# First loads of a two-block transformer kernel: which queue issues what, and when the small loads go out

## The reference

```
cos, sin = rope_tables(positions, HEAD_DIM)
mod = einsum('bd,ldm->lbm', silu(c), w_mod) + b_mod
for i in range(2):
    sh_m, sc_m, g_m, sh_f, sc_f, g_f = split(mod[i], 6)
    h = x * (1 + sc_m) + sh_m
    y = even_mixer(h, cos, sin, ...) if i == 0 else odd_mixer(h, cos, sin, ...)
    x = layer_norm(ALPHA * x + (1 + g_m) * y, ...)
    h = x * (1 + sc_f) + sh_f
    x = layer_norm(ALPHA * x + (1 + g_f) * swiglu(h, ...), ...)
```

## Time and profile before

| | us |
|---|---|
| median of 3 runs | 1142.61 (1140.88 to 1143.27) |
| the profiled execution, device time | 1144.01 |
| its span in the profile | 1142.7 |
| TensorE busy | 1124.9 (98%) |
| VectorE busy | 842.5 (74%) |
| ScalarE busy | 627.6 (55%) |
| GpSimd busy | 81.1 (7%) |
| loads through SP's queue | 230.32 MB |
| loads through GpSimd's queue | 0.31 MB |

### The profile page before, as it was taken

How to read it: one execution, slowest core, us unless ns; L and a number is a source line. 1 busy time by engine, 2 the same in 40 slices (tenths; PEclk the granted TensorE clock), 3 DMA queues, 4 the chain that set the end, 5 groups by cost and what they waited for, 6 DMA issues and landing times.

```text
span 1142.7 us, 24990 instructions
## 1 busy us (share of the span) xinstructions
PE 1124.9 (98%) x10534; PEld 1079.2 (94%) x10534; DVE 842.5 (74%) x1429; ACT 627.6 (55%) x1075; POOL 81.1 (7%) x103
## 2 busy tenths in 40 slices
PE   8999999999999999999999999999999999999998
PEld 6998799999998999999999999999999999999987
DVE  5698879988876888897575589578565677676643
ACT  3467556645435588666444455734645566555542
POOL 3000013000012000111000034100000000000000
PEclk9999999999999999999999999999999999999999
DMA  9977755899997643566655642843345463655540
GB/s 322 381 235 275 245 176 180 301 327 306 313 313 242 202 148 116 182 217 219 219 185 166 212 149 75 259 149 113 109 150 185 148 221 102 213 189 183 197 170 37
DMA packets 194687, 232.22 MB, mean 203 GB/s; under 512 B 4083, under 2 KB 169555, under 8 KB 194576
## 3 DMA queue, kind: packets, MB, share of 16 engines
q1 hardware_dynamic: 193984, 230.32, 60.6%
q0 software_dynamic: 592, 0.31, 0.2%
HBM read 229.56 MB, written 1.05 MB: 202 GB/s over the span
## 4 chain that ended last, share of the span: by engine, by line
PE 91%; DVE 4%; DMA 2%; issue 1%; ACT 1%; POOL 0%; SPq 0%; DVEq 0%
PE ps L154 90%; PE ps L157 2%; DMA XR<-in_x_dram 1%; DVE hL L196 1%; DVE wlo L187 1%; DMA raw<-in_w_in_even_dram 1%; DVE T L187 1%; DMA MW<-in_w_mod_dram 0%; DVE LT L187 0%; DVE T L196 0%; POOL T L187 0%; DVE XA L193 0%; DVE MR L196 0%; DVE ST L199 0%; ACT RD L166 0%
## 5 line engine op out<-in xcount | busy, mean ns | idle before, releaser
L187 DVE TENSOR_TENSOR wlo<-raw,whi 128x1024 fp32r<-128x1024 f32 (+1 forms) x346 | 409.9, 1206 | 162.3 <-ACT whi L166 161.0
L154 PE MATMUL ps<-hH,whi 128*128 128x256 f32 (+3 forms) x1792 | 517.2, 289 | 2.2 <-DVE hL L196 1.9
L154 PE MATMUL ps<-hH,wlo 128*128 128x256 f32 (+3 forms) x1792 | 504.6, 282 | 1.1 <-DVE wlo L187 1.1
L154 PE MATMUL ps<-hL,whi 128*128 128x256 f32 (+3 forms) x1792 | 505.0, 282 | 0.0
L166 ACT ACTIVATE whi<-raw 128x1024 fp32r<-128x1024 f32 (+1 forms) x346 | 349.5, 1033 | 193.3 <-PE ps L154 131.7
L154 PEld LDWEIGHTS ps<-hH,whi 128*128 128x128 f32 x1792 | 337.8, 189 | 8.8 <-issue 4.5
L154 PEld LDWEIGHTS ps<-hH,wlo 128*128 128x128 f32 x1792 | 338.1, 189 | 1.3 <-DVE wlo L187 1.3
L154 PEld LDWEIGHTS ps<-hL,whi 128*128 128x128 f32 x1792 | 338.4, 189 | 0.4
L154 PE MATMUL ps<-uL,whi 128*128 128x256 f32 x352 | 99.2, 282 | 0.0
L154 PE MATMUL ps<-uH,whi 128*128 128x256 f32 x352 | 99.0, 281 | 0.0
L154 PE MATMUL ps<-uH,wlo 128*128 128x256 f32 x352 | 98.4, 280 | 0.0
(11 more groups left out here) (314 smaller groups left out, 1614.4 us busy)
## 6 DMA issues: line engine op xcount, KB each, us to landing
MW<-in_w_mod_dram SPq DMA_DIRECT2D x47, 1024.0 KB, 6.9
raw<-in_w_up_dram SPq DMA_DIRECT2D x44, 1024.0 KB, 5.5
raw<-in_w_in_dram SPq DMA_DIRECT2D x36, 1024.0 KB, 5.0
raw<-in_w_down_dram SPq DMA_DIRECT2D x27, 1024.0 KB, 6.2
raw<-in_w_gate_dram SPq DMA_DIRECT2D x22, 1024.0 KB, 7.3
raw<-in_w_in_odd_dram SPq DMA_DIRECT2D x12, 1024.0 KB, 7.3
raw<-in_w_in_even_dram SPq DMA_DIRECT2D x8, 1024.0 KB, 9.6
raw<-in_w_down_dram SPq DMA_DIRECT2D x8, 768.0 KB, 6.7
```

Of the source, the lines that this page charges most:

```text
L154: return self.queued(self.e.matmul(out, lhsT, rhs, start=start, stop=stop, skip_group_check=True, **kw), length if pos is None else max(le ...
L187: return self.queued(self.e.tensor_tensor(out, a, b, op), 0.07 + cols(out) / self.RATE)
```

## The change

It has four parts. First, the loads of the vector, the identity and the bias are issued by ScalarE's queue (`k.act_dma`, a loader on the scalar engine) ahead of its table load, so SP's first instruction is the first modulation tile. Second, GpSimd's loads wait: the positions for the arrival of modulation tile 3, the meta tokens and the 16 parameter rows for tile 5. Third, the rotary tables are no longer written in one piece before the input is turned; they are a track that starts when the positions' load has been issued and yields between groups of instructions, so that they fall among the steps of `even`. Fourth, a `pace` ahead of the switch to the exponential table set makes sure that both sines are in the program before it, and `vectors` waits until the parameter rows have been issued.

```diff
 def begin(k):
-    pos_in = pool.dma(m.PI, D_["positions"].to_broadcast([128, S]), k.into["pos"])
-    k.meta_in = pool.dma(m.MTR, D_["meta_tokens_2"], k.into["meta"])
+    k.rows_in = k.meta_in = k.rope_tables = None
...
-    for g, r, src in rows_:
-        k.rows_in = pool.dma(RV[r:r + src.shape[0], g, 0:src.shape[1]], src, k.into["rows"])
-    c_in = sp.dma(RV[0:8, 0, :], vec(D_["c"]), k.into["c"])
-    ident_in = sp.dma(m.CST[:, 0:K_TRI], D_["cst"][:, 0:K_TRI], k.into["ident"])
-    bm_in = sp.dma(RV[0:96, 1, :], vec(D_["b_mod"]), k.into["bm"])
+    c_in = k.act_dma.dma(RV[0:8, 0, :], vec(D_["c"]), k.into["c"])
+    ident_in = k.act_dma.dma(m.CST[:, 0:K_TRI], D_["cst"][:, 0:K_TRI], k.into["ident"])
+    bm_in = k.act_dma.dma(RV[0:96, 1, :], vec(D_["b_mod"]), k.into["bm"])
...
+    def late_loads():
+        while 3 not in k.mod_loaded:
+            yield None
+        yield due(k.mod_loaded[3])
+        pos_in = pool.wait_ge(*k.mod_loaded[3]).dma(m.PI, D_["positions"].to_broadcast([128, S]), k.into["pos"])
+        start(k, rope_tables(pos_in))
+        while 5 not in k.mod_loaded:
+            yield None
+        yield due(k.mod_loaded[5])
+        k.meta_in = pool.wait_ge(*k.mod_loaded[5]).dma(m.MTR, D_["meta_tokens_2"], k.into["meta"])
+        for g, r, src in rows_:
+            rows_in = pool.dma(RV[r:r + src.shape[0], g, 0:src.shape[1]], src, k.into["rows"])
+        k.rows_in = rows_in
+
+    def rope_tables(pos_in):
+        ang, turns, r = m.ANG
...
+        yield due(pos_in)
+        dve.wait_ge(*pos_in).wait_ge(*ident_in).copy(ang, m.PI).settle().ts(ang, ang, inv, ALU.mult)
+        for out, turn_ in ((m.SIN, 0.0), (m.COS, 0.25)):
+            yield dve.clock
...
+            angle = dve.settle().ts(r, r, -3.1415925, ALU.max).inc()
+            yield due(angle)
+            sine = act.wait_ge(*angle).act(out, r, ACT.Sin, scale=sgn if out is m.SIN else 1.0).inc()
+        k.rope_tables = sine
...
+    start(k, late_loads())
     start(k, centred())
 def vectors(k, lane):
...
+    while k.rows_in is None:
+        yield None
     yield due(k.rows_in, k.meta_in)
 def even(k):
...
+    pace(k, lambda: due(k.rope_tables) if k.rope_tables else None)
     k.mods_soon = 8
     k.act.table(SET_EXP)
 def program(nc, args, out):
...
+        k.act_dma = Loader(nc.scalar, None)
```

More of the change, by code:

```diff
@@ L744, in begin @@
     k.b_mod = dve.inc()
[L746 to L760, removed]
@@ L761, in begin @@
-    k.rope_tables = sine
+    def late_loads():
[11 more added lines that the diff above has]
+        k.rows_in = rows_in
@@ new lines, in rope_tables @@
+    def rope_tables(pos_in):
+        ang, turns, r = m.ANG
+        inv, sgn = m.CST[:, K_INV:K_INV + 1], m.CST[:, K_SGN:K_SGN + 1]
+        sine = None
+        yield due(pos_in)
+        dve.wait_ge(*pos_in).wait_ge(*ident_in).copy(ang, m.PI).settle().ts(ang, ang, inv, ALU.mult)
+        for out, turn_ in ((m.SIN, 0.0), (m.COS, 0.25)):
+            yield dve.clock
+            dve.settle().ts(turns, ang, 1.0 / TWO_PI, ALU.mult, turn_, ALU.add)
+            dve.settle().ts(turns, turns, MAGIC, ALU.add).settle().ts(turns, turns, -MAGIC, ALU.add)
+            yield dve.clock
+            dve.settle()
+            if sine:
+                dve.wait_ge(*sine)
+            dve.stt(r, turns, -C1, ang, ALU.mult, ALU.add)
+            yield dve.clock
+            dve.settle().stt(r, turns, -C2, r, ALU.mult, ALU.add).settle().stt(r, turns, -C3, r, ALU.mult, ALU.add)
+            yield dve.clock
+            dve.settle().ts(r, r, turn_ * TWO_PI, ALU.add, 3.1415925, ALU.min)
+            angle = dve.settle().ts(r, r, -3.1415925, ALU.max).inc()
+            yield due(angle)
+            sine = act.wait_ge(*angle).act(out, r, ACT.Sin, scale=sgn if out is m.SIN else 1.0).inc()
+        k.rope_tables = sine
```

## The result

| | before | after |
|---|---|---|
| median, us | 1142.33 (1140.88 to 1143.27) | 1150.38 (1148.07 to 1152.81, 4 runs) |
| ratio, 95% interval | | 1.0074 [1.0061, 1.0086] |
| profiled execution, us | 1144.01 | 1148.07 |
| its span, us | 1142.7 | 1146.8 |

The changed kernel is slower by 0.7%, outside the predicted range. A second measurement of it gave 1150.01 against 1142.39, 1.0069 [1.0054, 1.0084]. The profiled execution of after is the fastest of its four, the one of before lay over its median, so the spans of the two traces differ by only 4.1 of the 8 us. One execution of a later kernel, h2, took 1360.71 us at a mean granted clock of 0.751 and is left out of that kernel's ratio.

A forecast was written before the change was run, and what follows sets the result against it. TensorE, busy 1124.9 of 1142.7 us, was taken as the bound, with a late useful start. Terms -1.2 - 1.0 + 0.4 + 0.2 = -1.6 took 1142.6 to 1141.0 us; range 1138.8 to 1144.2.

The forecast's parts named there:

- SP begins earlier, GpSimd's loads leave the head: At the start: SP issues 1.33 us earlier, GpSimd's absence gives 1.0; input lands at 13.2 (12.2 to 14.2).
- TensorE's own queue set the transposes: At the head: TensorE's queue, not the input's landing, sets the transposes' start, 14.06 instead of 15.55; at most 1.49 us gained.
- The delay of the identity: At the head: identity delayed 0.3 us beside the large loads (0 to 1.7); transposes start at 14.4, term -1.2.
- the transpose of `c` after 4: Sign at the head: `c` transposed after 4 us would show the first term wrong.
- The second gain: Between input transposes and first triple: both `LT` made once copies are; triple at T + 5.1 instead of T + 6.13, -1.0.
- The tables: Rotary tables moved into the steps: VectorE's idle mostly covers them; +0.4 us (-0.3 to +6.8).
- The small loads come back: After tiles 3 and 5: returning DMA time delays weights of s=2 and s=3; +0.2 us (0 to +1.98).
- Elsewhere 0, with 1 us either way: Rest of the kernel: tracks fall differently on all engines; 0, with 1 us either way.
- Everything through: Head and steps: identity not delayed, wait at s=1 gone, tables wholly hidden; -2.8 us to 1139.8; chance 0.24.
- Given back: Steps: pace set by loads or VectorE, so s=0's gain is lost waiting at s=1 and s=2; 1142.6; chance 0.15.
- The two issuers hold each other up: At the head: ScalarE's bias issue stands behind SP's held input issue, delaying `ones`; about 1143.9 us; chance 0.15.

The follow-up runs named there:

- h2: g4 with 2 instead of 5 products of `ones` behind the bias; 1141.21 us, ratio 0.9988.
- e2: The changed kernel with vector, identity and bias issued by SP as before; 1147.38 us, ratio 1.0035.
- e6: The changed kernel, with SP waiting for the identity before issuing the first modulation tile; single time 1146.12 us.
- h1: The same kernel as e6, timed over several runs; 1148.30 us, ratio 1.0057.
- h3: f1 with VectorE's order `LT`, `LT`, `hL`, `hL` at s=0 instead of `LT`, `hL`, `LT`, `hL`; 1141.76 us, ratio 0.9995.
- i1: h2 with h3's VectorE order at s=0; 1140.44 us, ratio 0.9973.
- e4: The kernel before with only the rotary tables moved among the steps, all loads issued as before; 1147.94 us, ratio 1.0039.
- f2: The kernel before with the rotary tables among the steps, everything else held in the order of before; 1146.49 us, ratio 1.0028.
- f5: The kernel before with its loads unchanged, but instructions in the order of e3; 1146.92 us, ratio 1.0039.
- f3: f2 plus late positions, meta tokens and parameter rows, in nearly the order of before; 1145.61 us, ratio 1.0025.
- e3: The kernel before with only the meta tokens and 16 parameter rows waiting for modulation tile 5; 1145.42 us, ratio 1.0023.
- g0: The changed kernel measured again, word for word; 1150.01 us, ratio 1.0069.
- e1: The kernel before with only vector, identity and bias moved to ScalarE's queue; 1145.17 us, ratio 1.0018.
- g4: f1 with the positions loaded as one 1 KB row and spread to the partitions by one TensorE product; 1142.96 us, ratio 1.0007.
- f1: The kernel before with late meta tokens and parameter rows, every engine kept in the order of before; 1141.89 us, ratio 0.9990.
- g2: f1 with the positions issued by SP behind the bias; 1141.58 us, ratio 0.9990.

## Why the prediction was wrong, step by step

**SP begins earlier, GpSimd's loads leave the head: right, and too small.** Landing 13.2 was forecast, 11.6 measured. SP's issue of the input took 1.70 instead of 4.19. And TensorE's own queue set the transposes, as argued: in after and in e2 they wait for nothing in front of them.

**The delay of the identity: this step failed first.** I took 0.3 with an upper bound of 1.7, from its bytes at half the rate and from the bias. It was 3.1 (transpose of `c` at 6.39 against 3.29). 81 KB are little, but with 2 MB beside them they took 4.9 us to land, and 1.9 without (e6). Before the change nothing large ran beside them, so the rows I had could not bound it; the bias, which landed 3.7 after its issue, was the nearest and still too low. The sentence on what would be wrong ("the transpose of `c` after 4") was the one that came true. In the time it is 1.9 (h1) to 2.8 (e2). The drop of `ones` x10 from 3.62 to 2.59 hid a part: the transposes came at 15.80, not 17.

The Trainium skill ("DMA: Bandwidth & Descriptors", "Issuing engines are not separate DMA queues") holds here: ScalarE's packets run on the same 16 engines as SP's, 11.3% beside 96.2%. I read it as saying that only issue time changes. What that means for a small load, the case shows: on another queue it no longer runs ahead of the large ones but beside them.

**The second gain: half right.** I said that both `LT` can be made as soon as the copies are. I overlooked that VectorE's order is static: its second `LT` is written behind the first `hL`, which waits for ScalarE (0.82 of idle at 20.09 in after, as in the earlier trace rows). The gain was T + 6.13 to T + 5.75, 0.4 instead of 1.0. h3 and i1 show that the reordered version does give T + 5.2.

**The tables: mis-sized.** I took +0.4 within -0.3 to +6.8. The wait of 0.30 at s=1 went, as I said it would, and one of 1.1 came at s=2 (1.8 in e2, where the head was earlier). With the order that goes with it the move costs 5.5 (e4, by the ratio 4.5); f2, where nothing else moves but more of the tables stand ahead of s=1, costs 3.8, and its profile has 2.4 more waiting for `hL` and 2.7 lost at the lower clock behind that wait. I had seen that ten of 18 instructions stand ahead of the `LT` of s=2 and priced them by the one wait of 0.30 shown before. A chain that TensorE already waited 0.3 for has no cover for 3.8 us of work, and I had no term for what a wait does to the clock.

**The small loads come back:** +0.2 was taken, 0.3 more waiting for `MW` measured. Right. SP also spent 10.38 us at 24.98 issuing two loads of weights, which I read as a full ring, as I did for the input before.

**"Elsewhere 0, with 1 us either way": the other large failure.** The `QS`, `oL`, `MR` and `T` waits are 3.4 us in after that no term of mine holds. That an order alone can cost 4.3 with every load in place f5 shows, for an order that isn't the one of after. I had the order of both kernels: three roundings ahead of the table load where one stood could be read there, and 2 x 1.0 us ahead of a `QS` for which TensorE waits is a term.

**Everything through** (1139.8) fell. **Given back** fell by its number (1142.6), but one of its two mechanisms is what happened: in e2 and f3 the triple comes 1.9 and 2.9 earlier, and `hL` is waited for 1.8 and 2.8 behind VectorE's static order. The other, the loads, is not it: with the tables ahead of the steps, i1 begins `QS,KS` 2.8 earlier than before. **The two issuers hold each other up** (1143.9) was the case on the slow side, and it fell too, as a mechanism: ScalarE's issues took 0.61, 0.36 and 0.44 beside SP's, and 0.58, 0.36 and 0.44 in h1, where SP issued nothing; SP's third issue began at 1.84 without a gap. Its form, a late small load that delays the `ones`, resembles what happened, but it was landing and not issuing that was late. The rule in the Trainium skill ("Perfetto Trace Analysis", "DMA Instruction — HWDGE (DVE, Sync)") that a sequencer locks the generator shows as no hold-up over 0.03 us in these runs. The case that I had in mind, the bias issued behind an input that is held, wasn't met: the bias was issued at 1.77, the input at 1.84 and in 1.70 us.

**The range** didn't fit its own chances: it was said to leave out 2 in 10, while the chances beside it put less than 0.15 outside. No case stood for a time over 1145.5.

**How it adds up.** e4, e2 and after are steps from one kernel to the other. The tables among the steps, with their order: +5.5 (before to e4). The late positions, meta tokens and rows: -0.6 (e4 to e2), within the noise. The three loads on ScalarE's queue: +2.8 (e2 to after). By the ratios it is 4.5, -0.5 and about 4. So of the 8 us some 5 lie in the moved tables and the order written with them, and some 3 in the late identity. How the 5 split between the tables' own time and the order stays open: f2 gives 3.8 for the tables in the order of before, but at other places than in after, and f5 and e3 price another order. The parts also overlap, since an engine that is waited for anyway hides the next delay. The half of the median difference that the profiled pair doesn't hold is in part the granted clock: 1.7 us of it are before's stretch at 0.50, and g0, with two such stretches and 1.1 more in the head, is 8.4 over before in its span.

## What to carry to other kernels

A small load on which the first instruction depends should be issued ahead of the large ones, and nothing large should be in flight beside it; another queue doesn't give it priority. Where a program writes its order from estimates, compare the order of every engine over the whole kernel after a change, hold it fixed to measure the change itself, and price each reordering near a place where the bottleneck engine waits. Idle time of an engine in a stretch is cover only for work that stands behind the instruction that is waited for. Before two profiles are subtracted, compare their granted clock: here one stretch at half rate in one of them hid 1.7 us.

## What was not expected of the hardware

- The identity's 81 KB landed after 1.9 to 2.0 us with nothing large beside them and after 4.7 to 4.9 beside two loads of 1 MB, the bias after 1.8 (e6) and 9.1 with three queues at work (e1).
- A record of `ones` takes 0.49 us early (2.93 for six at 3.46 in before) and 0.25 later (1.99 for eight at 18.36), a factor of two, with a granted clock shown as 1.00 in both places. The ten records between took 2.42 (g4) to 4.53 us (e1), and 2.59 and 3.87 in two executions of the changed kernel. In h2, with three products fewer, the four records that remain took 2.08, the first tile took 1.94 instead of 1.08 and the next `ones` 1.46 instead of 1.13: removing products moved the slowness to the next ones. This alone makes the head differ by up to 2 us.
- Behind a wait of TensorE the granted clock fell to 0.50 in some executions: while TensorE was at work never in the profiles of after, e6, h2 and i1, once in those of before, e1, e2, e3, f1, f5, g2, g4, h1 and h3, twice in e4, f2, f3 and g0. A stretch is 1.7 us of TensorE's time; the long one of f2 cost 2.7.
- The row of 256 positions copied to 128 partitions took 3.5 to 7.9 us to land on GpSimd's queue in these profiles and 5.6 on SP's; as one row of 1 KB it took 2.0 to 2.1.
